# Four places for the probabilities of one-map heads, and a paired order of heads in the last two mixers

## The reference, cut to what matters

```python
def memory_attention(q, k, v):
    scale = q.shape[-1] ** -0.5
    s = jnp.einsum('bshd,bmhd->bhsm', q, k).astype(jnp.float32) * scale
    p = jax.nn.softmax(s, axis=-1).astype(v.dtype)
    return jnp.einsum('bhsm,bmhd->bshd', p, v)

...
        o_a = moba_attention(qa, ka, va).reshape(B, S, G)
...
        o_m = memory_attention(qm, km, vm).reshape(B, S, G)

        y = jnp.concatenate([o_a, o_h, o_m], axis=-1) * jax.nn.silu(z)
        x = x + y @ w_out[l]
```

## Time and profile before

| what | us |
|---|---|
| runs of before, median (lowest, highest) | 1543.81 (1542.79, 1544.06) |
| the profiled execution, device time | 1543.93 |
| its span, first to last instruction | 1542.0 |
| PE busy in the span | 1498.4 (97%) |
| DVE busy | 1170.6 (76%) |
| ACT busy | 764.2 (50%) |
| mean granted clock | 0.997 |

### The profile page before, as it was taken

One profiled execution on the slowest core, in us unless ns is written; L12 is line 12 of the kernel. 1 busy time (PEld: TensorE's weight loads), 2 busy tenths in 40 slices (PEclk: granted clock), 3 DMA queues, 4 the chain that ended last, 5 costly groups with the idle time before them and its releaser, 6 DMA issues.

```text
span 1542.0 us, 23913 instructions
## 1 busy us (share of the span) xinstructions
PE 1498.4 (97%) x9958; PEld 1344.4 (87%) x9958; DVE 1170.6 (76%) x1390; ACT 764.2 (50%) x935; POOL 99.9 (6%) x70
## 2 busy tenths in 40 slices
PE   7999999999999999999998999999999989999988
PEld 6888899988888888888987888888999869999967
DVE  7878768756887778787677688777779677589774
ACT  5433456445433453334545543345564674555662
POOL 2000010011000010000100100001213001003000
PEclk9999999999999999999999999999999999999999
DMA  7555535213655555555441365554444214634302
GB/s 269 213 194 191 166 139 188 83 56 149 222 186 197 181 174 208 185 178 206 169 163 57 135 218 191 188 177 168 178 164 141 108 54 167 216 137 162 112 28 82
DMA packets 51888, 246.76 MB, mean 160 GB/s; under 512 B 4619, under 2 KB 5771, under 8 KB 27718
## 3 DMA queue, kind: packets, MB, share of 16 engines
q1 hardware_dynamic: 50662, 238.29, 43.9%
q0 software_dynamic: 1120, 6.96, 1.2%
HBM read 244.18 MB, written 1.05 MB: 159 GB/s over the span
## 4 chain that ended last, share of the span: by engine, by line
PE 80%; DVE 10%; ACT 6%; issue 2%; DMA 0%; POOL 0%; SPq 0%; DVEq 0%; ACTq 0%
PE ps L1149 21%; PE ps L1151 10%; PE ps L1072 9%; PE ps L1074 9%; PE ps L1073 9%; PE ps L1202 8%; PE ps L1203 4%; PE ps L1359 4%; ACT w_hi L1613 2%; DVE w_lo L1939 1%; ACT work L1826 1%; PE ps L1507 1%; PE ps L1496 1%; DVE act_two L2047 1%; ACT act_two L1691 1%
## 5 line engine op out<-in xcount | busy, mean ns | idle before, releaser
L1613 ACT ACTIVATE w_hi<-raw 128x2048 fp32r<-128x2048 f32 x186 | 355.2, 1913 | 387.1 <-PE ps L1151 270.5
L1939 DVE TENSOR_TENSOR w_lo<-raw,w_hi 128x2048 fp32r<-128x2048 f32 x179 | 409.6, 2291 | 138.8 <-ACT w_hi L1613 136.4
L1149 PE MATMUL ps<-act_two,w_hi 128*128 128x512 f32 x1408 | 445.2, 398 | 2.6 <-DVE xn L1948 1.3
L1072 PE MATMUL ps<-act_two,w_hi 128*128 128x256 f32 x1088 | 319.2, 293 | 4.0 <-DVE act_two L2186 2.9
L1151 PEld LDWEIGHTS ps<-act_two,w_lo 128*128 128x128 f32 x1408 | 265.8, 189 | 63.2
L1074 PE MATMUL ps<-act_two,w_lo 128*128 128x256 f32 x1088 | 307.7, 283 | 0.0
L1073 PE MATMUL ps<-act_two,w_hi 128*128 128x256 f32 x1088 | 307.7, 283 | 0.0
L1151 PE MATMUL ps<-act_two,w_lo 128*128 128x256 f32 x1408 | 277.9, 279 | 0.0
L1149 PEld LDWEIGHTS ps<-act_two,w_hi 128*128 128x128 f32 x1408 | 215.6, 190 | 5.4 <-DVE xn L1948 1.7
L1072 PEld LDWEIGHTS ps<-act_two,w_hi 128*128 128x128 f32 x1088 | 208.5, 192 | 9.6 <-issue 5.6
L1073 PEld LDWEIGHTS ps<-act_two,w_hi 128*128 128x128 f32 x1088 | 208.6, 192 | 4.4 <-issue 4.3
(11 more groups left out here) (294 smaller groups left out, 2063.7 us busy)
## 6 DMA issues: line engine op xcount, KB each, us to landing
raw<-panels SPq DMA_DIRECT2D x184, 1024.0 KB, 4.8
raw<-panels SPq DMA_DIRECT2D x80, 512.0 KB, 4.9
raw<-panels SPq DMA_DIRECT2D x8, 256.0 KB, 5.8
table<-tab POOLq DMA_DIRECT2D x1, 1472.0 KB, 9.0
table<-tab POOLq DMA_DIRECT2D x1, 1216.0 KB, 5.5
xn<-x_in SPq DMA_DIRECT2D x4, 256.0 KB, 4.8
work<-mem_in POOLq DMA_DIRECT2D x1, 1024.0 KB, 9.4
xn<-mem_in POOLq DMA_DIRECT2D x1, 1024.0 KB, 5.0
```

The lines of the kernel that those rows point to most:

```text
L1072: pe.matmul(o, l[0], r[0], start=start, stop=False, skip_group_check=shared)
L1149: pe.matmul(grid(ps[:, bank + half], 2), w[half][0], act_two[:, slots[c]], start=c == 0, stop=False)
L1613: nc.scalar.activation(w_hi[:, s], raw[:, s], ACT.Copy).then_inc(panel_hi, 1)
L1939: tt(w_lo[:, s], raw[:, s], w_hi[:, s].bitcast(F32), ALU.subtract).then_inc(panel_lo, 1)
```

## The change

One-map heads get four places: `place(unit)` gives `(i % 2, i // 2 % 2)`, and `place_user` names the last head before that used that place; mask_max waits for that head's turn_p, in place of the head two before. The room is the one that two-map heads use, so no memory is added; exp, divide and turn_p address the place. This holds for every one-map head, the dilated ones among them: their order stays as it was, and mask_max of dil 2 and dil 3 now waits for turn_p of dif 2 and dif 3.

`paired_heads` is written anew. There are six pairs, the four causal and two of memory heads. Step p holds the maxima and exps of pair p, the norm steps, scores of pair p + 1, attends of pair p - 2, and the divisions, turn_p and p_cols of pair p - 1. gate_out 0 and 1, y_splits and, for l = 1, turn_back and rows_back stand in given steps of this list rather than in chains of their own. The number of instructions on each engine stays the same, and no transfer moves.

```diff
@@ -402,24 +402,21 @@
 
 def paired_heads(l):
 
-    out = [[] for _ in range(16)]
-    pair = lambda p, *steps: [(e, k, ((f"moba{l}", h),)) for e, k in steps for h in (2 * p, 2 * p + 1)]
+    units = [(f"moba{l}", h) for h in range(8)] + [(f"matt{l}", h) for h in range(4)]
+    two = lambda p, *steps: [(e, k, (u,)) for e, k in steps for u in units[2 * p:2 * p + 2]] if 0 <= p < 6 else []
     norm = lambda kind, *groups: [("pe" if kind == "cn_sum" else "dve" if kind == "cn_use" else "act", kind, ((f"sq{l}", g),)) for g in groups]
-    out[0] += pair(0, ("pe", "scores")) + [("act", "evacuate", (f"in2_{l}", 19))] + norm("cn_sq", 0, 1) + norm("cn_sum", 0, 1)
-    for p in range(4):
-        a, b, c = 2 * p, 2 * p + 1, 2 * p + 2
-        out[a] += pair(p, ("dve", "mask_max"), ("act", "exp"))
-        if p in (0, 1):
-            out[a] += norm("cn_rstd", p)
-        if p in (1, 2):
-            out[a] += norm("cn_use", p - 1)
-        out[b] += pair(p + 1, ("pe", "scores")) if p < 3 else [("pe", "scores", ((f"matt{l}", h),)) for h in (0, 1)]
-        out[b] += pair(p, ("pe", "turn_p"), ("dve", "divide"), ("act", "p_cols"))
-        out[c] += pair(p, ("pe", "attend"))
-    single = lambda h, *steps: [(e, k, ((f"matt{l}", h),)) for e, k in steps if 0 <= h < 4]
-    for r in range(4 + 2):
-        out[8 + r] += single(r, ("dve", "mask_max"), ("act", "exp")) + single(r - 1, ("dve", "divide"))
-        out[8 + r] += (single(r + 1, ("pe", "scores")) if r else []) + single(r - 1, ("pe", "turn_p"), ("act", "p_cols")) + single(r - 2, ("pe", "attend"))
+    gate = lambda g: [("dve", "gate_out", ((f"moba{l}", g),))]
+    out = [two(0, ("pe", "scores")) + [("act", "evacuate", (f"in2_{l}", 19))] + norm("cn_sq", 0, 1) + norm("cn_sum", 0, 1)]
+    for p in range(6 + 2):
+        step = two(p, ("dve", "mask_max"), ("act", "exp"))
+        step += norm("cn_rstd", p) if p < 2 else []
+        step += norm("cn_use", p - 1) if p in (1, 2) else []
+        step += two(p + 1, ("pe", "scores")) + two(p - 2, ("pe", "attend"))
+        step += two(p - 1, ("dve", "divide"), ("pe", "turn_p"), ("act", "p_cols"))
+        step += gate(0) if p == 3 else gate(1) if p == 5 else []
+        step += y_splits(l, 0) if p == 5 else y_splits(l, 2) if p == 6 else []
+        step += [("pe", "turn_back", (p - 2,)), ("act", "rows_back", (p - 2,))] if l and p in (2, 3, 4, 5) else []
+        out[-1:] = [out[-1] + step] if p == 0 else [out[-1], step]
     return out
 
 
@@ -433,14 +430,10 @@
     chains = [hgrn,
               [[]] * n + rounds(NORM_COLS, qk + [(f"ho{l}", 0), (f"ho{l}", 1)]),
               [[]] * (n + 2) + rounds(ROPE, qk),
-              [[]] * h + paired_heads(l),
-              [[]] * (h + 6) + [[("dve", "gate_out", ((f"moba{l}", 0),))], [], [], [("dve", "gate_out", ((f"moba{l}", 1),))]],
-              [[]] * (h + 13) + [y_splits(l, 0), y_splits(l, 2)]]
+              [[]] * h + paired_heads(l)]
     if l == 0:
         load, *stats = mem_norm(1)
         chains += [[[]] * (h + 1) + [[load]]]
-    if l:
-        chains += [[[]] * (h + 7) + sum(([[("pe", "turn_back", (b,)), ("act", "rows_back", (b,))], []] for b in range(PAIRS)), [])]
     places = [n + r for r in BESIDE_2]
     if l:
         places[:4] = [0, 1, 2, 2]
@@ -828,6 +821,18 @@
                 return 1 if two(unit) or (i and two(att_list[i - 1])) else 2
             return m if two(unit) else i % 2
 
+        def place(unit):
+
+            i = att_index[unit]
+            return (i % 2, 0) if len(atts[unit][0]) == 2 else (i % 2, i // 2 % 2)
+
+        def place_user(unit):
+
+            i, (b, m) = att_index[unit], place(unit)
+            both = lambda u: len(atts[u][0]) == 2
+            users = [u for u in att_list[:i] if place(u)[0] == b and (both(u) or both(unit) or place(u)[1] == m)]
+            return users[-1] if users else None
+
         def spans(full):
 
             return [(0, 256), (256, 512)] if full else [(0, 128), (128, 384)]
@@ -1527,7 +1532,7 @@
                 pe.wait_ge(dve_done, at("dve", "divide", unit))
                 if i >= 2:
                     pe.wait_ge(act_done, at("act", "p_cols", att_list[i - 2]))
-                p, bank = probs[:, i % 2, 0], ps[:, 2 + i % 2]
+                p, bank = probs[:, place(unit)[0], place(unit)[1]], ps[:, 2 + i % 2]
                 second = SEQ if full else P
                 pe.transpose(bank[:, 0:P], p[:, 0:P], ident)
                 pe.transpose(bank[:, P:SEQ], p[:, second:second + P], ident)
@@ -1821,8 +1826,9 @@
                 act.wait_ge(dve_done, at("dve", "mask_max", unit))
                 for m in range(len(maps)):
                     for q, (a, b) in enumerate(spans(full)):
-                        p = probs[:, i % 2, m, a:b]
-                        c = 2 * m + q
+                        m_ = place(unit)[1] + m
+                        p = probs[:, i % 2, m_, a:b]
+                        c = 2 * m_ + q
                         ins = nc.scalar.activation(p, p, ACT.Exp, bias=nmax[i % 2][:, c:c + 1], scale=-1.0,
                                                    accum_out=dens[i % 2][:, c:c + 1])
                 step(ins)
@@ -2217,12 +2223,13 @@
                 maps, _, _, full, mask, _, k, _ = atts[unit]
                 i = att_index[unit]
                 dve.wait_ge(pe_done, at("pe", "scores", unit))
-                if i >= 2:
-                    dve.wait_ge(pe_done, at("pe", "turn_p", att_list[i - 2]))
+                if place_user(unit):
+                    dve.wait_ge(pe_done, at("pe", "turn_p", place_user(unit)))
                 for m in range(len(maps)):
                     for q, (a, b) in enumerate(spans(full)):
-                        to, s = probs[:, i % 2, m, a:b], ps[:, score_bank(unit, m), a:b]
-                        low = nmax[i % 2][:, 2 * m + q:2 * m + q + 1]
+                        m_ = place(unit)[1] + m
+                        to, s = probs[:, i % 2, m_, a:b], ps[:, score_bank(unit, m), a:b]
+                        low = nmax[i % 2][:, 2 * m_ + q:2 * m_ + q + 1]
                         if full:
                             ins = ts(to, s, -k, None, ALU.mult, ALU.min, accum_out=low)
                         else:
@@ -2232,7 +2239,8 @@
             def divide(unit):
                 maps, _, _, full, _, times, _, _ = atts[unit]
                 i = att_index[unit]
-                p, den = probs[:, i % 2], dens[i % 2]
+                m = place(unit)[1]
+                p, den = probs[:, i % 2, m:], dens[i % 2][:, 2 * m:]
                 dve.wait_ge(act_done, at("act", "exp", unit))
                 if times is not None:
                     for q, (a, b) in enumerate(spans(full)):
```

## The result

The changed kernel takes 1548.96 us (median of 7 runs, 1547.16 to 1552.76), the kernel before in the same measurement 1544.3 (median of 7, 1542.79 to 1545.9). The ratio is 1.003 with a 95% interval of 1.0019 to 1.0041: 4.7 us slower, where 1543.0 was forecast with a range up to 1548.1. The profiled execution of the changed kernel took 1549.38 us with a span of 1547.5; that of before had 1543.93 and 1542.0.

A forecast was written before the change was run, and what follows sets the result against it. PE was taken to hold 80% of the chain, with gains only where it waits for softmax steps. -2.8 (dilated heads) + 1.5 (mixer 0) + 0.5 (mixer 1) = -0.8 gave 1543.0 us; range 1538.8 to 1548.1.

The forecast's parts named there:

- Dilated heads: First block: the four places remove DVE waits (1.1 us) and the low clock behind them (1.7 us); -2.8 us.
- I expect the clock to hold: Dilated heads: PE's gaps shrink to about 0.7 us each, so the fall after 846.5, worth 1.7 us, goes away.
- Heads of the mixers at full clock: Last mixers 0 and 1: new order followed step by step, +1.5 us (+1.1 to +1.9) and +0.5 (+0.1 to +0.9).
- The named cause: Last mixers: y_lo 0 waits for ACT ahead of memory heads 2 and 3's divisions; mixer 0 ends 1.1 us later before handovers.
- Clock in the openings: Last mixers: a PE gap of 1.7 us ahead of turn_p; a fall costs up to 1.7, counted as 0.
- two rivals: The second and third rivals, which count a clock fall of 1.7 us in each last mixer's opening.
- The second rival: Last mixers: the clock falls in both openings, +2.6 us, 1546.4; chance 0.17.
- the third: Clock falls in both openings and the fall behind the dilated heads stays, +4.3 us, 1548.1; chance 0.12.
- The first rival: Last mixers: ACT sets the pace without gaps, -1.5 and -1.9 us; with -2.8 that is -6.2, 1537.6; chance 0.18.
- The fourth: Dilated heads: what DVE gains is lost on ACT, so that term is 0; +2.0 us, 1545.8; chance 0.10.

The follow-up runs named there:

- the filled kernel of before: Kernel before with 3 constant matmuls behind the scores of dil 3 and 4 behind the attend of dil 0; 1543.38 us, ratio 0.9997.
- filler ahead of out1: Kernel before with the four places alone, plus 4 and 5 constant matmuls behind the attends of dil 2 and dil 3; 1540.9 us, ratio 0.9971.
- the kernel with the small filler: Changed kernel with 3 and 4 constant matmuls behind the scores of heads 3 and 5 in both last mixers; 1545.47 us, ratio 1.0009.
- these two kernels: Changed kernel with fillers in the openings and y_hi, y_lo behind all heads, 1541.82 us; the same with cn_use behind the divisions too, 1540.67 us.
- places, old order: Kernel before with the four places alone, its order of steps untouched; 1540.99 us, ratio 0.9983.
- everything undone and filled: Changed kernel with y_hi, y_lo behind all heads, cn_use behind the divisions, 3 constant matmuls in each of PE's two opening gaps; 1540.67 us, ratio 0.9980.
- the kernel with cn_use moved: Changed kernel with cn_use of the two sq groups behind the divisions of the pair, in place of ahead of them; 1546.65 us, ratio 1.0018.
- the two kernels with fillers elsewhere: Kernel before with constant matmuls in the dilated heads, 1543.38 us; the four places alone with constant matmuls ahead of out1, 1540.9 us.
- one of 3.9 us: Changed kernel with 6 and 9 constant matmuls behind the scores of heads 3 and 5 in both last mixers; 1544.87 us, ratio 1.001.

## Why the prediction was wrong, step by step

**Dilated heads: right, and given back.** -2.8 was forecast, 1.1 for waits and 1.7 for the clock; measured are -2.72, of which 1.09 and 1.63 by the filled kernel of before. turn_p of dil 2 was forecast at 845.6 and stands at 846.01, 845.54 less the later start. The step that failed is "I expect the clock to hold". It held up to 850, and fell at the first out1 matmuls, behind gaps of 1.22 and 1.48 us that the trace of before has as well, there without a fall. That returned 1.49 us. The prediction took the clock's loss as a thing of one place, and priced its end there; it didn't look for the next gap on PE. With the places and no filler ahead of out1 the clock fell there in 8 of 9 profiled executions, with that filler in neither of two; the one that held it without a filler shows that the gaps alone do not decide it.

**Heads of the mixers at full clock: right in size.** +1.5 and +0.5 were forecast, +1.61 and +0.34 measured, by the kernel with the small filler. The named cause holds too: y_lo ahead of the divisions is 1.50 and 0.89 us of it, cn_use ahead of the divisions 29.72 - 29.26 = 0.46 and 30.38 - 29.57 = 0.81 (these two kernels also differ in where the second filler stands, so a part of this may be the filler's). One thing was missed on the other side: the places gain 0.82 and 0.95 us in the mixers even in the old order.

Added up, mixer 0 is 28.79 (places, old order) + 0.47 (the rest of the new order) + 0.46 (cn_use) + 1.50 (y_lo) + 2.16 (clock) = 33.38 us, and mixer 1 is 29.98 - 0.41 + 0.81 + 0.89 + 2.25 = 33.52. The terms come from one profiled execution each; that kernels with the same steps agree (28.79 and 28.81, 29.26 twice, 29.57 twice, 29.98 twice) says how well.

**Clock in the openings: the step that made it wrong.** "I count 0 in the sum and 1.7 in two rivals." It was 2.16 and 2.25. The gap ahead of turn_p was foreseen (1.7 us; measured 1.00 and 1.35, because the scores of heads 4 and 5 came later than I had them, behind a gap of 0.91). Two things were wrong: that the likeliest case was a held clock, and the price, taken from a fall within 3.5 us, where this one lasted at least 6.45. (The trace of before has the fall not only once: there is another at 27 us, and one at its very end, where PE has no more work. Neither is longer than that at 846.5, so the price would have been the same.) The section that the prediction cites from the Trainium skill (page "TensorE: Matmul & The Clock Gate", section "HAM oscillation — how this bites in real kernels") tells of bursts of matmuls that are shorter than the waits between them. The rows agree that PE ran slow behind waits. But here the waits, 0.91 and 1.00 us, were short beside the work, 5.02 us of the 7.27 ahead of the fall, so the section does not cover this case, and the measurement decides.

**The rivals.** The second rival, the clock falling in both openings (1546.4), and the third, with the low clock behind the dilated heads as well (1548.1), describe what happened, the third nearly so: in place of staying at 846 the fall moved to 853. That the third's term for the dilated heads, -1.1, is close to the measured -2.72 + 1.49 = -1.23 is luck: the full gain was made and half of it lost again at another place. With the right price, -2.8 + 1.5 (out1) + 1.5 + 0.5 + 2.2 + 2.2 = +5.1, against 5.5 between the profiled executions and 4.7 between the medians. The first rival never showed: with everything undone and filled the stretches still were 29.3 and 29.6. The fourth was wrong.

What stays open: why the clock falls in one execution and not in another at the same steps. The heads dif 2 and dif 3, the same in all kernels, had a low clock near 825 to 830 in 4 of the 13 profiled executions here, out1 held it once without a filler, and the kernel with cn_use moved had it in one mixer of two. In those dif heads it cost nothing: from the scores of dif 2 to out1 35.91 us passed with it and 35.92 without.

## What to carry to other kernels

Steps that are brought forward on one engine leave a gap behind them, and where TensorE has the gap, the price is not the gap: here the half clock behind it cost 2.2 us, for gaps of 1.0 and 1.35. A fall that the trace of before shows is no upper bound for that price: it had none longer than 3.5 us, and the new order had falls of at least 6.45. Look for the next gap when one is closed, and test it with a few idle matmuls, which change the clock and no step's order. And before a new order of steps is written for a freed resource, run the old order with the resource freed: here that alone was 0.17% faster than before, and the same places with the new order were 0.3% slower.

A step that only the end needs (y_lo) belongs behind the steps that others wait for, even when its input is ready early, because every engine here works strictly in the order of the list and its wait is theirs (1.50 and 0.89 us here).

## What the runs showed of the hardware

The clock fell behind short waits, with PE far from idle: PE was busy for 5.02 of the 7.27 us ahead of the fall in mixer 0, and no wait there was longer than 1.00 us. Once low, it stayed at 0.50 for at least 6.45 us although PE was busy for 6.44 of them; the fall at out1 with the places alone, with PE just as full, lasted 3.4 us. In the old order no opening of a mixer had a fall, in 8 of 8 (before, the places alone, and the two kernels with fillers elsewhere); in the new order without fillers 7 of 8 had one, with fillers in the gaps none of 10. A filler of 2.1 us in all (0.94 and 1.16) was enough here, and one of 3.9 us (1.60 and 2.27), longer than the gaps, held up turn_p by itself.
